# A two-layer hybrid decoder step on one core: warm-up matmuls, order of block 0, tail stores and cache loads

## The chip, the core and the metric

The kernel runs on one core of a Trainium2 chip. The metric is the time of the device in microseconds (us), from the profiler's records or from timed executions.

## What is computed

One inference step of two layers for a prompt group (256 tokens) and a sample group (8 sequences of 4 tokens); both have the same weights and stand side by side as T = 288 columns. The model width is 1024.

```python
x = LN1(alpha*x + 0.5 * SwiGLU_1(x))          # D_FF = 2816
z = x @ w_in                                  # 1024 -> 6144: conv, LRU, query, three gates
y_conv = (cb * conv3(cc * cv)) @ conv_out
y_lru  = (rg_lru(conv4(lx)) * gelu(lg)) @ lru_out
y_att  = attention(q, k_mem, v_mem) @ att_out # 4 heads x 128, 256 memory tokens
m = sum_b sigmoid(g_b) * y_b
x = LN2(alpha*x + m @ w_o)
x = LN3(alpha*x + 0.5 * SwiGLU_2(x))
```

The prompt's keys and values are computed from mem_prompt; those of the samples come from caches, 8 tiles of keys and 8 of values for each layer, 128 x 1024 fp32 (512 KB) each. Outputs are the new x, the prompt's keys and values and the states of the convolutions and of the LRU.

## The kernel before, in words

**Blocks.** Every product with a weight is cut into blocks of 256 output channels; a block n is up to eight 128x256 weight tiles (1 MB), and the class Plan numbers them in the order of the work: F1 and D1 (first SwiGLU), Z (w_in 0 to 11), B (the three branches: gate block, then half-size projection block, four times for each branch), O, F2, D2. A product in fp32 is made of three in fp32r: high by high, high parts of the weights by low parts of x, low parts of the weights by high parts of x (products, L438 to L441). A block so costs 8 x 2 x 3 matmuls of 288 columns.

**Queues.** SP loads the block n into raw (load, L323 to L325) when the low parts of block n-2 are done (lo_ready). ScalarE casts a half block to its high part, whi (L733); VectorE subtracts, wlo (L1030). TensorE waits for lo_ready for each half block and counts pe_half, by one for each half block it has used: after block n it is 2n+2. Each engine works through its list strictly in the order written out in the code, so other vector and scalar work stands between the casts by hand.

**Start (block 0).** first_blocks (L456) does the first two blocks. Their first half is loaded in pieces of two tiles, as is x, on SP's and ScalarE's queues. ScalarE casts a pair of weight tiles, then a pair of x tiles (L742 to L749); VectorE makes the low parts of both (L1042 to L1048) and counts x_ready. TensorE first does eight matmuls of 8 and eight of 256 columns on zeros (L435), then for k = 0, 1, ... four products with xh (high and low weights), two with xl.

**Branches.** For each of the three branches b and four parts i, TensorE does gate(b, i), then project(b, i); with B = plan.at[l]["B"] the gate's block is B + 8b + 2i, the projection's one more. The samples' attention lies between: sample_scores(0 to 3) behind gate(0,1), sample_scores(4 to 7) behind gate(0,3), sample_values(0 to 3) behind project(1,1), sample_values(4 to 7) behind project(1,3). The cache tiles pass through four buffers, kv[b % 4]. Each use counts kv_used. The prompt's attention runs head by head in branch 1: prompt_transposes(i) behind gate(1,i), prompt_values(i) (L654) behind project(1,i). VectorE, for i = 0: the low half of block B+10 (gate_lo), then the copies L1463 of the samples' probabilities into pz, then L1466 (prt), on which prompt_values(0) waits. Ahead of gate(0,3)'s low half it has the LRU's L1410, L1412 and L1413.

**POOL's queue.** For each layer (L410 to L422) POOL sends sixteen cache loads (b = 0 to 7 keys, 8 to 15 values):

```python
for b in range(2 * NS):
    if b == 2:
        pool_e.wait_ge(conv_done, l + 1)
    if b >= BATCH:
        pool_e.wait_ge(kv_used, l * (2 * NS) + b - BATCH + 1)
    ...
    g.dma_start(kv[b % BATCH], cache).then_inc(kv_in[b % BATCH], 16)
    if b == BATCH - 1:
        g.memset(qz_flat, 0.0).then_inc(qz_zero, 1)
    if b == NS + BATCH - 1:
        pool_e.wait_ge(p_prob, l * AH + 1)
        for t in pz_flat:
            g.memset(t, 0.0).then_inc(pz_zero, 1)
```

**Tail.** After the last layer norm ScalarE writes tiles 0 to 4 of x (L866), VectorE tiles 5 to 7 (L1252, counted by y_last). SP stores tiles 0-1, 2-3 and 4-5 (L372), ScalarE's queue tiles 6-7 (L869).

Of the kernel before, what the change touches and what calls it, by code (L numbers as in the profile page):

```python
# [11 lines left out]
P = 128  # L12
HEAD = 128
BC = 256
# [2 lines left out]

ATANH_TERMS = 9
PITCH, SHIFT = 352, 24
WARM_NARROW, WARM_WIDE = 8, 8  # L20
ENDS_ON_ACT = 5

ROW_NAMES = ("ln1_g", "ln1_b", "ln2_g", "ln2_b", "ln3_g", "ln3_b", "conv_w", "lru_conv_w", "lru_conv_b",
# [68 lines left out]
def hybrid_decoder_step(nc, I, O, dims):  # L92
    L, NS, TS, TP, M, D, FF, CK, LK, AH = dims
    T = TP + NS * TS
    DC = LW = D // 2
    KD = D // P
    KB = DC // P
    KF = FF // P
# [30 lines left out]
    with ExitStack() as ctx:  # L129
# [3 lines left out]
        def sem(name):  # L133
            return ctx.enter_context(nc.semaphore(name))
# [99 lines left out]

        first_in = [sem("first_in0"), sem("first_in1"), sem("first_in2")]
        second_in = sem("second_in")
        first_hi, first_lo = sem("first_hi"), sem("first_lo")
        warm_ready = sem("warm_ready")
        hi_ready, lo_ready, pe_half, drained = sem("hi_ready"), sem("lo_ready"), sem("pe_half"), sem("drained")

# [80 lines left out]
        @block.sync  # L321
        def _(sp):
            def load(n, s, src):  # L323
                sp.wait_ge(lo_ready, 2 * n - 2)
                sp.dma_start(raw[:, s, 0:src.shape[1], :], src).then_inc(raw_full[s], 16)  # L325

            def fills(gap):
                for n, f in gap:
                    load(n, n % 2, fill_source(f))

            for l in range(L):
                at = plan.at[l]

                def ffn(k, f0, d0, gap):
                    if l == 0 and k == 1:
                        src = I["ffn1_wg"][0, 0]
                        for c, full in enumerate((*first_in, raw_full[0])):
                            sp.dma_start(raw[:, 0, 2 * c:2 * c + 2, :], src[:, 2 * c:2 * c + 2, :]).then_inc(full, 16)
                        src = I["ffn1_wu"][0, 0]
                        for (k0, k1), full in zip(halves(KD), (second_in, raw_full[1])):  # L340
                            sp.dma_start(raw[:, 1, k0:k1, :], src[:, k0:k1, :]).then_inc(full, 16)
                    else:
                        n = f0 - len(gap)
                        load(n, n % 2, I[f"ffn{k}_wg"][l, 0])
                        fills(gap)
                        load(f0 + 1, (f0 + 1) % 2, I[f"ffn{k}_wu"][l, 0])
                    with sp.Fori(1, PAIRS_F) as i:
                        for s, w in enumerate((f"ffn{k}_wg", f"ffn{k}_wu")):
                            load(f0 + 2 * i + s, (f0 + s) % 2,
                                 I[w][l, bass.ds(i, 1)].rearrange("o p k n -> p (o k) n"))  # L350
                    for b in range(3 * PAIRS_D):
                        j, c = divmod(b, 3)
                        load(d0 + b, (d0 + b) % 2, I[f"ffn{k}_wd"][l, j][:, 8 * c:8 * c + DK[c], :])

                ffn(1, at["F1"], at["D1"], gap(3 * l - 1) if l else ())
                for n, j, f in z_blocks(l):
                    load(n, n % 2, I["w_in"][l, j] if f is None else fill_source(f))
                for b, w in enumerate(("conv_out", "lru_out", "att_out")):
                    for i in range(PAIRS_D):
                        n = at["B"] + 8 * b + 2 * i  # L360
                        load(n, n % 2, I["w_in"][l, 12 + 4 * b + i])
                        load(n + 1, (n + 1) % 2, I[w][l, i])
                for j in range(PAIRS_D):
                    load(at["O"] + j, (at["O"] + j) % 2, I["w_o"][l, j])
                ffn(2, at["F2"], at["D2"], gap(3 * l + 1))


            for p in range(PAIRS_D - 1):
                sp.wait_ge(x_full, KD * (3 * L - 1) + min(2 * p + 2, ENDS_ON_ACT))
                if 2 * p + 2 > ENDS_ON_ACT:  # L370
                    sp.wait_ge(y_last, 2 * p + 2 - ENDS_ON_ACT)
                sp.dma_start(O["y"][:, 2 * p:2 * p + 2, :], x[:, 2 * p:2 * p + 2, :]).then_inc(y_out, 16)  # L372
            sp.wait_ge(k_out, 16 * L)
            sp.wait_ge(v_out, 16 * L)
            sp.wait_ge(col_out, 16 * L)
            sp.wait_ge(y_out, 16 * PAIRS_D)

        @block.gpsimd
        def _(pool_e):
# [17 lines left out]
            for l in range(L):  # L397
                if l > 0:
                    pool_e.wait_ge(bd_psum, l * 8)
                for j, w in enumerate(("lru_wa", "lru_wx")):  # L400
                    for e in range(2):
                        h = P // 2
                        g.dma_start(bd[e * h:(e + 1) * h, j, :, e * h:(e + 1) * h],
                                    I[w][l].rearrange("(k e) a b -> e a k b", e=2)[e]).then_inc(bd_in, 16)
                pool_e.wait_ge(fill_out, plan.fills_done(l, "k"))
                g.dma_start(O["p_mem_k"][l], kt[:, :, :]).then_inc(k_out, 16)
                pool_e.wait_ge(fill_out, plan.fills_done(l, "v"))
                g.dma_start(O["p_mem_v"][l], vt[:, :, :]).then_inc(v_out, 16)

                for b in range(2 * NS):  # L410
                    if b == 2:
                        pool_e.wait_ge(conv_done, l + 1)
                    if b >= BATCH:
                        pool_e.wait_ge(kv_used, l * (2 * NS) + b - BATCH + 1)
                    cache = I["cache_k" if b < NS else "cache_v"][l, b % NS]
                    g.dma_start(kv[b % BATCH], cache).then_inc(kv_in[b % BATCH], 16)
                    if b == BATCH - 1:
# [5 lines that stand above are left out]
                if l + 1 < L:  # L423
                    pool_e.wait_ge(kv_used, (l + 1) * (2 * NS))
                    g.dma_start(mem[:, :, :], I["mem"]).then_inc(mem_in, 16)
                pool_e.wait_ge(col_ready, l + 1)
                g.dma_start(O["cols"][l], cols[:, l]).then_inc(col_out, 16)

        @block.tensor
        def _(pe):  # L430
# [1 line left out]
            pe.wait_ge(consts, 7)  # L432

            pe.wait_ge(warm_ready, 1)
            for cols in (8,) * WARM_NARROW + (BC,) * WARM_WIDE:  # L435
                mm(ps[:, 7, 0:cols], hh[:, KF - 1, 0:P], hh[:, KF - 1, 0:cols], start=True, stop=True)

            def products(out, wh, wl, mh, ml, start, stop):  # L438
                mm(out, wh, mh, start=start, stop=False)  # L439
# [15 lines left out]

            def first_blocks(n):  # L456

                for s, k in ((s, k) for s in range(2) for k in range(KD)):
                    if (s, k) == (0, 0):
                        pe.wait_ge(xh_ready, 1)  # L460
                    elif s == 0:
                        pe.wait_ge(x_ready, k + 1)
                    if s == 0 and k % 2 == 0:
                        pe.wait_ge(lo_ready if k % 4 else first_lo, k // 4 + 1)
# [3 lines left out]
                    for t in range(2):  # L468
# [1 line left out]
                        c = slice(t * P, (t + 1) * P)  # L470
                        mm(out, whi[:, s, k, c], xh[:, k, :], start=k == 0, stop=False)  # L471
                        mm(out, wlo[:, s, k, c], xh[:, k, :], start=False, stop=False)  # L472
                    if (s, k) == (0, 0):
                        pe.wait_ge(x_ready, 1)
                    for t in range(2):
                        last = mm(ps[:, 2 * s + t, 0:T], whi[:, s, k, t * P:(t + 1) * P], xl[:, k, :],
                                  start=False, stop=k == KD - 1)
# [251 lines left out]
        def _(act):  # L729
# [14 lines left out]
            for c in range(PAIRS_D):  # L744
                p = slice(2 * c, 2 * c + 2)
                act.wait_ge((*first_in, raw_full[0])[c], 16)
                s_.copy(whi[:, 0, p, :], raw[:, 0, p, :]).then_inc(hi_ready if c % 2 else first_hi, 1)
                act.wait_ge(x_in[c], 16)
                s_.copy(xh[:, p, :], x[:, p, :]).then_inc(xh_ready, 2)  # L749
            for (k0, k1), full in zip(halves(KD), (second_in, raw_full[1])):  # L750
                act.wait_ge(full, 16)
                split(1, 1, k0, k1)
# [5 lines left out]
            for l in range(L):  # L758
# [77 lines left out]
                def norm(n, l, ln):  # L836
# [25 lines left out]
                    if not more:  # L862
                        gc = ROWS[f"ln{ln + 1}_g"]
                        for k in range(ENDS_ON_ACT):
                            act.wait_ge(normed, KD * q + k // 2 + 1)
                            s_.activation(x[:, k, :], y[:, k, :], ACT.Identity, bias=pts[:, l, bc + k:bc + k + 1],  # L866
                                          scale=pts[:, l, gc + k:gc + k + 1]).then_inc(x_full, 1)
                        act.wait_ge(y_last, KD - ENDS_ON_ACT)
                        s_.dma_start(O["y"][:, KD - 2:KD, :], x[:, KD - 2:KD, :]).then_inc(y_out, 16)  # L869
                        return  # L870
                    for k in range(KD):
                        act.wait_ge(normed, KD * q + k + 1)
# [151 lines left out]
        def _(dve):  # L1024
# [14 lines left out]

            dve.wait_ge(bd_zero, 1)  # L1040
            v.tensor_copy(hh[:, KF - 1, 0:BC], bd[:, 0, 0:2, :].rearrange("p k c -> p (k c)")).then_inc(warm_ready, 1)
            for c in range(PAIRS_D):  # L1042
                p = slice(2 * c, 2 * c + 2)
                dve.wait_ge(hi_ready if c % 2 else first_hi, c // 2 + 1)
                rest(wlo[:, 0, p, :], raw[:, 0, p, :], whi[:, 0, p, :]).then_inc(lo_ready if c % 2 else first_lo, 1)
                dve.wait_ge(x_in[c], 16)
                dve.wait_ge(xh_ready, 2 * c + 2)
                rest(xl[:, p, :], x[:, p, :], xh[:, p, :]).then_inc(x_ready, 2)  # L1048
            for h in range(2):
                lo(1, h)  # L1050
# [517 lines left out]
```

## Time and profile before

| | us |
|---|---|
| median of 3 runs | 1396.47 |
| lowest, highest | 1395.02, 1397.40 |
| the profiled execution | 1396.84 |
| its span | 1394.9 |
| TensorE busy (98% of the span) | 1373.7 |
| VectorE busy (64%) | 894.8 |
| ScalarE busy (48%) | 665.9 |
| POOL busy (2%) | 34.8 |

The span runs from the first to the last record of the profiled execution; its time has about 2 us more around it. Busy times are sums over an engine's instructions. DMA-issuing instructions are not counted as busy. Each instruction of the timeline has its start, its length, its line and, in brackets, how long the engine was idle before it and what ended that.

### The profile page before, as it was taken

To read this page: it belongs to the slowest core of one execution; us is meant where nothing else is said; L and a number is where in the kernel's file an instruction comes from. 1 tells how busy PE (TensorE), PEld (TensorE's weight loads), DVE (VectorE), ACT (ScalarE), POOL (GpSimd) and SP (SyncE) were. 2 spreads that over 40 slices of the span, in tenths; PEclk is the share of its full clock that TensorE was granted. 3 is DMA by queue.
4 is the path that set the end of the run, shared out by engine and by line. 5 is a ranking of instruction groups with operands and counts; after the bars stand their busy time and mean duration, and the time that the engine had idled before them with its cause. 6 is when DMAs were issued, how large, how long until landed. Compare 5 with 4: busy or idle time off the path is not lost.

```text
span 1394.9 us, 25447 instructions
## 1 busy us (share of the span) xinstructions
PE 1373.7 (98%) x10566; PEld 1357.2 (97%) x10566; DVE 894.8 (64%) x1180; ACT 665.9 (48%) x896; POOL 34.8 (2%) x68
## 2 busy tenths in 40 slices
PE   9999999999999999999999999999999999999996
PEld 8999999999899999999999999999998999999996
DVE  5555568496865885554685555585887568655444
ACT  5444446445444664444474444463544455544433
POOL 0100000000101000000000000000001000000000
PEclk9999999999999999999999999999999999999999
DMA  6654444755555454444445544446455453554441
GB/s 241 203 178 157 152 166 160 258 179 178 203 191 204 159 182 157 173 154 162 167 167 181 179 154 143 166 172 228 167 202 204 162 200 129 181 180 153 171 166 57
DMA packets 39998, 243.60 MB, mean 175 GB/s; under 512 B 4577, under 2 KB 4593, under 8 KB 16369
## 3 DMA queue, kind: packets, MB, share of 16 engines
q1 hardware_dynamic: 33264, 219.00, 45.0%
q0 software_dynamic: 5936, 22.01, 4.3%
q10 hardware_dynamic: 720, 1.47, 0.3%
q8 instruction: 59, 0.97, 0.3%
q14 instruction: 19, 0.15, 0.0%
HBM read 238.97 MB, written 3.50 MB: 174 GB/s over the span
## 4 chain that ended last, share of the span: by engine, by line
PE 91%; DVE 4%; DMA 3%; ACT 1%; issue 1%; DVEq 0%
PE ps L440 29%; PE ps L439 29%; PE ps L441 29%; DMA raw<-in_w_in 2%; DVE wlo L1030 1%; PE ps L527 1%; ACT whi L733 1%; PE ps L638 1%; PE ps L631 1%; PE ps L654 1%; PE ps L599 0%; PE ps L623 0%; DMA raw<-in_ffn_wg 0%; PE ps L471 0%; PE ps L472 0%
## 5 line engine op out<-in xcount | busy, mean ns | idle before, releaser
L1030 DVE TENSOR_TENSOR wlo<-raw,whi 128x1024 fp32r<-128x1024 f32 (+1 forms) x450 | 510.1, 1141 | 320.6 <-ACT whi L733 316.4
L733 ACT CAST whi<-raw 128x1024 fp32r<-128x1024 f32 (+1 forms) x446 | 437.2, 987 | 505.1 <-PE ps L441 382.9
L439 PE MATMUL ps<-xh,whi 128*128 128x288 f32 (+1 forms) x2144 | 635.6, 296 | 4.4 <-DVE wlo L1030 3.2
L440 PE MATMUL ps<-xl,whi 128*128 128x288 f32 (+1 forms) x2144 | 631.4, 294 | 0.0
L441 PE MATMUL ps<-xh,wlo 128*128 128x288 f32 (+1 forms) x2144 | 630.5, 294 | 0.0
L439 PEld LDWEIGHTS ps<-xh,whi 128*128 128x128 f32 x2144 | 404.4, 189 | 6.9 <-ACT pool L964 2.9
L440 PEld LDWEIGHTS ps<-xl,whi 128*128 128x128 f32 x2144 | 406.1, 189 | 0.7
L441 PEld LDWEIGHTS ps<-xh,wlo 128*128 128x128 f32 x2144 | 405.5, 189 | 0.0
L439 PE MATMUL ps<-hh,whi 128*128 128x288 f32 (+1 forms) x1088 | 322.0, 296 | 0.0
L440 PE MATMUL ps<-hl,whi 128*128 128x288 f32 (+1 forms) x1088 | 319.4, 294 | 0.0
L441 PE MATMUL ps<-hh,wlo 128*128 128x288 f32 (+1 forms) x1088 | 319.1, 293 | 0.0
L440 PEld LDWEIGHTS ps<-hl,whi 128*128 128x128 f32 x1088 | 206.1, 189 | 0.4
L439 PEld LDWEIGHTS ps<-hh,whi 128*128 128x128 f32 x1088 | 205.2, 189 | 1.2 <-issue 0.8
L441 PEld LDWEIGHTS ps<-hh,wlo 128*128 128x128 f32 x1088 | 205.7, 189 | 0.0
L1100 DVE SCALAR_TENSOR_TENSOR pool<-pool,ps 128x576 f32<-128x576 f32 x41 | 30.9, 753 | 49.9 <-ACT pool L774 49.9
L774 ACT ACTIVATE pool<-ps 128x576 f32<-128x576 f32 x41 | 26.7, 651 | 69.9 <-PE ps L441 69.9
L1106 DVE TENSOR_TENSOR pool<-pool,ps 128x576 f32<-128x576 f32 x44 | 33.1, 753 | 34.6 <-PE ps L441 34.6
L1030 DVE TENSOR_TENSOR hl<-pool,hh 128x576 f32 (+3 forms) x54 | 45.2, 844 | 0.9 <-ACT hh L819 0.2
L1146 DVE SCALAR_TENSOR_TENSOR y<-x,ps 128x576 f32<-128x576 f32 x18 | 13.6, 754 | 33.6 <-PE ps L441 33.6
L791 ACT CAST hh<-pool 128x576 f32 (+1 forms) x44 | 29.7, 675 | 3.2 <-DVE pool L1106 3.2
L860 ACT ACTIVATE xh<-y,pts 128x288 fp32r<-128x288 f32 x40 | 20.4, 532 | 18.9 <-DVE y L1221 18.4
L964 ACT ACTIVATE pool<-ps 128x576 f32<-128x576 f32 x24 | 15.6, 650 | 18.6 <-PE ps L441 18.6
(191 smaller groups left out, 747.5 us busy)
## 6 DMA issues: line engine op xcount, KB each, us to landing
raw<-in_w_in SPq DMA_DIRECT2D x48, 1024.0 KB, 4.9
raw<-in_ffn_wg SPq DMA_DIRECT2D x43, 1024.0 KB, 4.9
raw<-in_ffn_wu SPq DMA_DIRECT2D x43, 1024.0 KB, 4.9
raw<-in_ffn_wd SPq DMA_DIRECT2D x32, 1024.0 KB, 4.9
raw<-in_ffn_wd SPq DMA_DIRECT2D x16, 768.0 KB, 4.1
raw<-in_w_o SPq DMA_DIRECT2D x8, 1024.0 KB, 4.9
raw<-in_w_k_mem SPq DMA_DIRECT2D x4, 1024.0 KB, 5.5
raw<-in_w_v_mem SPq DMA_DIRECT2D x4, 1024.0 KB, 5.7
```

The lines of the kernel that those rows point to most:

```text
L439: mm(out, wh, mh, start=start, stop=False)
L440: mm(out, wh, ml, start=False, stop=False)
L441: return mm(out, wl, mh, start=False, stop=stop)
L527: return mm(ps[:, 4 + kind, 0:T], ones[:, :], tile, start=first, stop=last)
L733: s_.copy(whi[:, s, k0:k1, :], raw[:, s, k0:k1, :]).then_inc(hi_ready, 1)
L774: s_.activation(th[:, :, :], ps[:, 0:2, 0:T], ACT.Tanh, scale=0.5).then_inc(ffn_tanh, 1)
L791: s_.copy(hh[:, bass.ds(i * 2, 2), :], hf[:, :, :]).then_inc(ffn_hi, 1)
L860: return s_.activation(out[:, k, :], y[:, k, :], ACT.Identity, bias=pts[:, l, bc + k:bc + k + 1])
L964: s_.activation(tg[:, :, :], ps[:, 0:2, 0:T], ACT.Tanh, scale=0.5).then_inc(gate_tanh, 1)
L1030: return v.tensor_tensor(out, full, high.bitcast(F32), sub)
L1100: v.scalar_tensor_tensor(sg[:, :, :], th[:, :, :], 1.0, ps[:, 0:2, 0:T], add, mult).then_inc(drained, 1)
L1106: v.tensor_tensor(hf[:, :, :], sg[:, :, :], ps[:, 2:4, 0:T], mult).then_inc(drained, 1)
```

## The change

It has four parts.

1. The warm-up on zeros is seventeen matmuls of 256 columns in place of eight of 8 and eight of 256.
2. In block 0 VectorE casts the first pair of x tiles, as soon as it has landed, in place of ScalarE; TensorE does the four products of high parts for k = 0, 1 first, then the four with the low weights, then the four with the low x; from k = 2 on the order is as it was.
3. The last stores are regrouped: SP stores tiles 0-1, 2-3, 5-6 and 7, ScalarE's queue tile 4.
4. From b = 4 on, of each group of four cache loads the second, third and fourth also wait for pe_half to reach 2n+4, 2n+5 and 2n+6, n being block B+2, B+6 or B+10 for the three groups. 2n+4 is the end of the projection behind gate block n, 2n+5 the middle of the next gate block, 2n+6 its end.

```diff
-WARM_NARROW, WARM_WIDE = 8, 8
+WARM = 17
...
+            def leave(k0, k1):
+                sp.dma_start(O["y"][:, k0:k1, :], x[:, k0:k1, :]).then_inc(y_out, 16)
+
+            for k in range(0, ENDS_ON_ACT - 1, 2):
+                sp.wait_ge(x_full, KD * (3 * L - 1) + k + 2)
+                leave(k, k + 2)
+            sp.wait_ge(y_last, KD - 1 - ENDS_ON_ACT)
+            leave(ENDS_ON_ACT, KD - 1)
+            sp.wait_ge(y_last, KD - ENDS_ON_ACT)
+            leave(KD - 1, KD)
...
+                def spread(b):
+
+                    n = plan.at[l]["B"] + (2, 6, 10)[b // BATCH - 1]
+                    return 2 * n + (0, 4, 5, 6)[b % BATCH]
+
                 for b in range(2 * NS):
                     if b == 2:
                         pool_e.wait_ge(conv_done, l + 1)
                     if b >= BATCH:
                         pool_e.wait_ge(kv_used, l * (2 * NS) + b - BATCH + 1)
+                        if b % BATCH:
+                            pool_e.wait_ge(pe_half, spread(b))
...
-            for cols in (8,) * WARM_NARROW + (BC,) * WARM_WIDE:
-                mm(ps[:, 7, 0:cols], hh[:, KF - 1, 0:P], hh[:, KF - 1, 0:cols], start=True, stop=True)
+            for _ in range(WARM):
+                mm(ps[:, 7, 0:BC], hh[:, KF - 1, 0:P], hh[:, KF - 1, 0:BC], start=True, stop=True)
...
-                for s, k in ((s, k) for s in range(2) for k in range(KD)):
-                    if (s, k) == (0, 0):
-                        pe.wait_ge(xh_ready, 1)
-                    elif s == 0:
+                pe.wait_ge(first_xh, 1)
+                pe.wait_ge(first_hi, 1)
+                for part in range(3):
+                    if part > 0:
+                        pe.wait_ge((None, first_lo, x_ready)[part], part)
+                    for k in range(2):
+                        for t in range(2):
+                            mm(ps[:, t, 0:T], (wlo if part == 1 else whi)[:, 0, k, t * P:(t + 1) * P],
+                               (xl if part == 2 else xh)[:, k, :], start=k + part == 0, stop=False)
+                for s, k in [(0, k) for k in range(2, KD)] + [(1, k) for k in range(KD)]:
+                    if s == 0:
                         pe.wait_ge(x_ready, k + 1)
...
-                act.wait_ge(x_in[c], 16)
-                s_.copy(xh[:, p, :], x[:, p, :]).then_inc(xh_ready, 2)
+                if c > 0:
+                    act.wait_ge(x_in[c], 16)
+                    s_.copy(xh[:, p, :], x[:, p, :]).then_inc(xh_ready, 4 if c == 1 else 2)
...
-                        act.wait_ge(y_last, KD - ENDS_ON_ACT)
-                        s_.dma_start(O["y"][:, KD - 2:KD, :], x[:, KD - 2:KD, :]).then_inc(y_out, 16)
+                        act.wait_ge(x_full, KD * q + ENDS_ON_ACT)
+                        s_.dma_start(O["y"][:, ENDS_ON_ACT - 1:ENDS_ON_ACT, :],
+                                     x[:, ENDS_ON_ACT - 1:ENDS_ON_ACT, :]).then_inc(y_out, 16)
...
+            dve.wait_ge(x_in[0], 16)
+            v.tensor_copy(xh[:, 0:2, :], x[:, 0:2, :]).then_inc(first_xh, 1)
             for c in range(PAIRS_D):
```

## Rows read from the trace of the kernel before

**Rows 1.** The page, busy time of TensorE: us, share of the span, instructions.
```profile
PE 1373.7 (98%) x10566; PEld 1357.2 (97%) x10566; DVE 894.8 (64%) x1180; ACT 665.9 (48%) x896; POOL 34.8 (2%) x68
```

**Rows 2.** TensorE's waits: us in total, times, longest us.
```profile
PE ps L439 <- DVE wlo L1030: 3.2, 2, 2.7
...
PE ps L654 <- DVE pool L1466: 1.9, 2, 1.7
```

**Rows 3.** Timeline of TensorE: start, us, line, form, idle before and releaser.
```profile
355.10 0.37 PE L439 MATMUL ps<-xh,whi 128*128 128x288 f32 x1 [2.73 <-DVE wlo L1030]
...
378.14 0.45 PE L654 MATMUL ps<-pool,vt 128*128 128x256 f32 x1 [0.22 <-DVE pool L1466]
...
1039.92 0.37 PE L439 MATMUL ps<-xh,whi 128*128 128x288 f32 x1 [0.45 <-DVE wlo L1030]
...
1064.51 0.45 PE L654 MATMUL ps<-pool,vt 128*128 128x256 f32 x1 [1.72 <-DVE pool L1466]
```

**Rows 4.** Timeline of SP, issue of blocks B+6 and B+10 in layer 0.
```profile
344.79 0.33 SPq L325 DMA_DIRECT2D raw<-in_w_in  x1
...
369.86 0.33 SPq L325 DMA_DIRECT2D raw<-in_w_in  x1
```

**Rows 5.** DMA issues, last us to landing; from 338, 362, 370, 391, 1026, 1055 us.
```profile
raw<-in_w_in SPq DMA_DIRECT2D x1, 1024.0 KB, 7.8
...
kv_more<-in_cache_v POOLq DMA_DIRECT2D x1, 512.0 KB, 3.4
...
raw<-in_w_in SPq DMA_DIRECT2D x1, 1024.0 KB, 4.8
...
raw<-in_lru_out SPq DMA_DIRECT2D x1, 512.0 KB, 4.4
kv_more<-in_cache_v POOLq DMA_DIRECT2D x1, 512.0 KB, 6.2
...
raw<-in_w_in SPq DMA_DIRECT2D x1, 1024.0 KB, 6.9
...
raw<-in_w_in SPq DMA_DIRECT2D x1, 1024.0 KB, 6.3
```

**Rows 6.** Timeline of TensorE, first product of gate(0,2), layer 0.
```profile
342.81 0.29 PE L439 MATMUL ps<-xh,whi 128*128 128x288 f32 x1
```

**Rows 7.** Timeline of VectorE and ScalarE ahead of gate(0,3), layer 0.
```profile
351.35 0.81 DVE L1413 TENSOR_SCALAR pool<-pool 128x1248 f32<-128x1248 f32 x1
353.73 1.23 DVE L1030 TENSOR_TENSOR wlo<-raw,whi 128x1024 fp32r<-128x1024 f32 x1 [1.57 <-ACT whi L733]
...
352.58 1.04 ACT L733 CAST whi<-raw 128x1024 fp32r<-128x1024 f32 x1 [8.95 <-DMA raw<-in_w_in]
```

**Rows 8.** Timeline of VectorE ahead of gate(0,3), layer 1.
```profile
1037.03 0.81 DVE L1413 TENSOR_SCALAR pool<-pool 128x1248 f32<-128x1248 f32 x1
```

**Rows 9.** Timeline of TensorE, the first transpose behind gate(1,0), layer 0.
```profile
373.92 0.38 PE L690 MATMUL ps<-ident,pool 128*128 128x128 f32 x2
```

**Rows 10.** Timeline of POOL, two cache loads and the zeroing of pz.
```profile
363.60 1.05 POOL L416 DMA_DIRECT2D pool<-in_cache_v  x2
373.89 1.84 POOL L422 MEMSET pool<- 128x1024 f32 x2 [9.23 <-DVE pool L1457]
```

**Rows 11.** Timeline of VectorE ahead of prompt_values(0), both layers.
```profile
376.91 0.48 DVE L1463 COPY pool<-ps 128x128 f32<-128x128 f32 x2
...
1062.14 1.22 DVE L1030 TENSOR_TENSOR wlo<-raw,whi 128x1024 fp32r<-128x1024 f32 x1 [3.47 <-ACT whi L733]
```

**Rows 12.** Timeline of TensorE and VectorE in the first 10 us.
```profile
3.12 3.75 PE L436 MATMUL ps<-hh 128*128 128x8 f32 x16 [3.12 <-DVE hh L1041]
...
8.86 0.76 DVE L1030 TENSOR_TENSOR xl<-x,xh 128x576 fp32r<-128x576 f32 x1
...
9.78 0.30 PE L471 MATMUL ps<-xh,whi 128*128 128x288 f32 x1
```

**Rows 13.** Timeline of the last store.
```profile
1391.58 0.36 ACTq L869 DMA_DIRECT2D out_y<-x  x1
```

More of the change, by code:

```diff
@@ L236, in hybrid_decoder_step @@
         second_in = sem("second_in")
-        first_hi, first_lo = sem("first_hi"), sem("first_lo")
+        first_hi, first_lo, first_xh = sem("first_hi"), sem("first_lo"), sem("first_xh")
         warm_ready = sem("warm_ready")
@@ L365, in _ @@
                 ffn(2, at["F2"], at["D2"], gap(3 * l + 1))
[L368 to L372, printed above, removed]
+            def leave(k0, k1):
[7 more added lines that the diff above has]
+            leave(KD - 1, KD)
             sp.wait_ge(k_out, 16 * L)
@@ L375, in _ @@
             sp.wait_ge(col_out, 16 * L)
-            sp.wait_ge(y_out, 16 * PAIRS_D)
+            sp.wait_ge(y_out, 16 * (PAIRS_D + 1))
         @block.gpsimd
@@ L472, in first_blocks @@
                         mm(out, wlo[:, s, k, c], xh[:, k, :], start=False, stop=False)
-                    if (s, k) == (0, 0):
-                        pe.wait_ge(x_ready, 1)
                     for t in range(2):
@@ L1045, in _ @@
                 rest(wlo[:, 0, p, :], raw[:, 0, p, :], whi[:, 0, p, :]).then_inc(lo_ready if c % 2 else first_lo, 1)
-                dve.wait_ge(x_in[c], 16)
-                dve.wait_ge(xh_ready, 2 * c + 2)
+                if c == 0:
+                    dve.wait_ge(first_xh, 1)
+                else:
+                    dve.wait_ge(x_in[c], 16)
+                    dve.wait_ge(xh_ready, 2 * c + 2)
                 rest(xl[:, p, :], x[:, p, :], xh[:, p, :]).then_inc(x_ready, 2)
```

## The prediction

> **What bounds the kernel now.** I read the page, then who waited for whom on TensorE, then the timelines around the longest waits, then the DMA landings there, then the two ends. TensorE is busy for 1373.7 us of a span of 1394.9 us [rows 1], so only what shortens one of its few waits can move the end. Apart from the start, where it has no work yet, the list of waits has two entries that this change can reach: 3.2 us in two waits of a weight product (L439) for the low parts (L1030), and 1.9 us in two waits of the prompt's first value product (L654) for the vector engine's copy L1466 [rows 2]. The timeline places them: 2.73 us before 355.10 in layer 0 and 0.45 us before 1039.92 in layer 1, both at the gate block w_in[15] (block B+6); 0.22 us before 378.14 and 1.72 us before 1064.51, both before prompt_values(0) [rows 3].
>
> The wait at 355.10 goes back over casts to a weight load: w_in, issued at 344.79 [rows 4], landed 7.8 us later, where the same 1 MB load took 4.8 us in a quiet stretch [rows 5]. Just ahead of it the POOL queue had sent four cache tiles of 512 KB back to back; a single one in a quiet stretch lands after 3.4 us [rows 5]. In layer 1 the same load took 6.9 us behind the same four tiles, and the load of block B+10 (gate(1,1)) took 6.3 us against 4.8 us in layer 0 [rows 5].
>
> **The change part by part.** The sum is made against the profiled execution, 1396.84 us, which lies 0.37 us above the median of 1396.47.
>
> *Block B+6, layer 0.* b=4 still goes out at once; b=5 now waits for project(0,1), which ends at 342.81, b=6 for the first half of gate(0,2), which takes 3.1 us (TensorE's 1373.7 us over its 10566 matmuls is 0.13 us each, and a half block has 24), b=7 for its end, another 3.1 us [rows 1, 6]. So at 344.79 one tile has mostly moved, and two come behind the weights. The price of 512 KB that goes ahead is 4.8 - 3.4 = 1.4 us at most (512 KB more in a load). The weights should land 4.8 to 6.2 us after 344.79, at 349.6 to 351.0; the cast takes 1.04 us, to 352.05 at the latest. VectorE isn't free until L1413 ends at 351.35 + 0.81 = 352.16; its 1.23 us for the low half ends at 353.4, and TensorE starts 0.14 us behind it as before (354.96 to 355.10), at 353.53 [rows 7]. That is 1.57 us earlier, wherever in that interval the load lands; what is late next is L1413. I take **-1.5**, between -1.57 and 0.
>
> *Block B+6, layer 1.* VectorE's L1413 ends at 1037.84 there [rows 8] and would allow 1039.2, but TensorE is only idle for 0.45 us [rows 3]. Where does b=5 fall? TensorE is ready for the block at 355.10 - 2.73 = 352.37 in layer 0, 9.56 us after project(0,1) ends, so in layer 1, ready at 1039.47, that end is at 1029.9. The load is issued at 1039.92 - 2.53 (landing to start, as in layer 0) - 6.9 = 1030.5. So b=5 goes out 0.6 us ahead of the weights, and 4.8 + 1.4 = 6.2 us instead of 6.9 is the likely landing, 0.7 us sooner. I take **-0.4**, between -0.45 and 0.
>
> *Block B+10.* Today all four value tiles are sent at about 362.6, and the weights issued at 369.86 [rows 4] find the queues empty: 4.8 us. After it b=11 follows the end of gate(1,0) at 373.92 [rows 9], b=10 the end of its first half, 3.1 us before that, at 370.8 or 0.9 us behind the weights, and b=9 its start, at 367.6 (6.3 us before its end). If the tile behind the weights shares their bandwidth, they land up to 1.4 us later, and TensorE, idle for 0.22 us already, waits for all of it. The nearest row is a 512 KB weight load at 391.5 with a cache tile 0.3 us behind it: the weights took 4.4 us, the tile 6.2 instead of 3.4 [rows 5]. The later one paid. So I take **+0.3** in layer 0, between 0 and +1.4. In layer 1 the landing of 6.3 us leaves 1.5 us to win, all of it inside the 1.72 us wait. By the layer 0 row minus the same 0.3 that is 1.2; since I can't show that the tiles caused the excess, **-1.1**, between -1.5 and 0.
>
> Beside this stands a rule of the Trainium skill, "DMA: Bandwidth & Descriptors", section on queues, rings and completion order: each DMA engine takes turns between the queues that have work, packet by packet. By it the tile behind the weights does slow them, and the term is +1.4; the row at 391.5 speaks against it. It is a rival below.
>
> *The zeroing of pz (L422).* It stands behind b=11 in POOL's order, so the new wait of b=11 holds it. Today it starts at 373.89 and takes 1.84 us for both halves [rows 10]. Now: gate(1,0) ends at 373.92, about 0.4 us for the last matmul and the wake, 0.53 us for the issue (POOL's row of two tiles takes 1.05 [rows 10]), 1.84 us: about 376.8. VectorE reaches its consumer, L1463, at 376.91 [rows 11]. In layer 1 the gate's end lies as far ahead of TensorE's being ready for L654 as in layer 0 (377.92 - 373.92 = 4.0), at 1062.79 - 4.0 = 1058.8, and the same 2.9 us give 1061.7; VectorE's low half there runs from 1062.14 to 1063.4 [rows 11], or to 1062.2 if the load is 1.2 us faster. Cost **0**, with a margin of 0.1 and 0.5 us; up to +0.6 without it. The value tiles themselves are wanted only after project(1,1), over 10 us later. The third group of tiles (b=12 to 15) has no TensorE wait near it, now or with tiles sent later: 0.
>
> *Block 0.* The sixteen warm-up matmuls took 3.75 us [rows 12]; seventeen wide ones take about as long (1/16 of it, 0.2 us, more), to about 7.0. VectorE casts the first x (its subtraction on the same 576 columns takes 0.76) while ScalarE casts the weights. The twelve products of k = 0, 1 can then start at about 7.0. But k = 2 waits for x_ready 3, the low parts of the second pair of x, which VectorE has at 8.86 + 0.76 = 9.62 behind transfers that aren't touched; today the first product of k = 2 starts at 9.78 [rows 12]. So the twelve products end earlier, and a short wait takes their place. **-0.05**; where the clock comes up later than in this execution, an earlier start is worth up to 0.5, and a change of its timing could cost as much.
>
> *Tail.* Today the last two tiles (288 KB) go out together at 1391.58, behind the third vector op [rows 13]. Now only the last one (144 KB) does, but SP must first issue tiles 5 and 6, two issues in one queue. The same bytes are in flight in the last 3 us. I take **-0.15**, between -0.5 and +0.3.
>
> Sum: -1.5 - 0.4 + 0.3 - 1.1 - 0.05 - 0.15 = -2.9. From 1396.84 that is 1393.9; against the median, with which the result is compared, 1396.47 - 2.9 = **1393.6**.
>
> **The rivals.**
> 1. *The queues take turns* (the skill's rule). B+6 in layer 0 still gains its 1.5, since VectorE is the limit up to a landing of 6.2 us. In layer 1 the load meets b=5 and b=6: -0.2. B+10 costs +1.4 in layer 0 and, at 6.2 instead of 6.3 us, gains 0.1 in layer 1. Sum -1.5 - 0.2 + 1.4 - 0.1 - 0.2 = -0.6: 1395.9. For it: a rule; against it: the tile that paid at 391.5.
> 2. *The excess isn't the tiles'.* A load of block B+10 took 6.3 us some 6 us behind its tiles, so a part of such excess may be scatter. Then only B+6 in layer 0 gains: -1.5 - 0.2 = -1.7: 1394.8.
> 3. *Slower: pz_zero comes last.* If POOL's issue of b=11, the fourth tile in its ring, is held up, or wakes late, each us beyond 376.9 and 1062.2 stands in front of L1463, L1466 and so of L654, in both layers. It decides from 0.1 us on; to lose 2.9 + 2.8 us it has to be about 2.9 us late in each layer, which gives 1396.47 + 2.8 = 1399.3. Against it: POOL's rows of two tiles are 1.05 us wherever I look.
> 4. *More than forecast*: all bounds good, -1.57 - 0.45 - 1.5 - 0.5 - 0.5 = -4.5: 1392.0.
>
> **How the numbers follow.** A measurement of this kernel can tell 0.2%, 2.8 us, from no change, so the forecast stands right at that border. The forecast's case has 0.58, of which a bit over 0.4 beyond -2.8; rival 1 0.18, rival 2 0.12, rival 3 0.05, rival 4 0.07. Faster 0.47, within 0.2% 0.48, slower 0.05. The range takes in rival 4 and rival 1 with half a us of scatter between executions: 1391.6 to 1396.5.
>
> **What would show it.** Right: the L439 wait of 2.73 us shrinks to about 1.2 us and follows L1413 directly; the 0.45 us wait is gone; w_in of B+6 lands in under 6.2 us; L654 waits for under 0.8 us in each layer; b=5, 6, 7 each alone on POOL's timeline. Rival 1: w_in of B+10 at 6 us or more in both layers, the wait before L654 over 1.2 us in both. Rival 3: L1463 is released by the memset L422. In block 0 a short wait of TensorE before k = 2, ended by the low part of x, and k = 2 at 9.7. The prediction is wrong if TensorE's waits shrink as said and the time doesn't, or if the start or the tail moves by over 0.6 us.

## The result and the profile after

The changed kernel takes 1400.08 us (median of 20 runs), the kernel before 1394.86 us in as many runs beside it: a ratio of 1.003, interval 1.002 to 1.0039. It is **slower by 0.3%**, outside the predicted range (1391.6 to 1396.5) and on the side that had a chance of 0.05: a gain of 2.9 us was forecast, and the medians lie 5.2 us apart the other way. A second series of the changed kernel (g4_after below) gave 1.0023, interval 1.001 to 1.0036. Its profiled execution took 1399.52 us with a span of 1397.6; the page gives the busy times, which stand against [rows 1]:

```profile
PE 1373.6 (98%) x10567; PEld 1356.4 (97%) x10567; DVE 895.4 (64%) x1181; ACT 666.9 (48%) x895; POOL 35.4 (3%) x68
```

TensorE is busy as long as before, so the time went into its waits. Its list of waits (us in total, times, longest), against [rows 2]; L1049, L1490 and L1481 are the lines that were L1030, L1466 and L1457, and L451, L671 and L662 were L439, L654 and L645:

```profile
PE ps L671 <- DVE pool L1490: 4.0, 2, 2.4
...
PE ps L451 <- DVE wlo L1049: 2.8, 2, 2.4
...
PE ps L662 <- DVE pool L1481: 0.3, 1, 0.3
```

Before, the first two stood at 1.9 and 3.2. TensorE's timeline places them, against [rows 3] (start, us, line, form, idle before and releaser):

```profile
355.70 0.37 PE L451 MATMUL ps<-xh,whi 128*128 128x288 f32 x1 [2.35 <-DVE wlo L1049]
...
380.98 0.45 PE L671 MATMUL ps<-pool,vt 128*128 128x256 f32 x1 [2.42 <-DVE pool L1490]
...
1057.71 0.40 PE L451 MATMUL ps<-xh,whi 128*128 128x288 f32 x1 [0.42 <-DVE wlo L1049]
...
1067.07 0.45 PE L671 MATMUL ps<-pool,vt 128*128 128x256 f32 x1 [1.56 <-DVE pool L1490]
```

Of the four waits, the one at block B+6 in layer 0 fell from 2.73 us to 2.35, not by 1.5. The one in front of prompt_values(0) in layer 0 rose from 0.22 to 2.42. The 0.45 us at block B+6 in layer 1 are gone, and 0.42 us have come at the next block but one, gate(1,0). The last is 1.72 before and 1.56 after. The landings explain them. First the cache loads on POOL's timeline, layer 0 (b = 5, 6 and 7, b = 9 and 11, and the zeroing of pz):

```profile
344.51 0.53 POOL L428 DMA_DIRECT2D kv_more<-in_cache_k  x1 [4.32 <-PE ps L453]
...
347.64 0.53 POOL L428 DMA_DIRECT2D pool<-in_cache_k  x1 [2.60 <-PE ps L453]
...
350.77 0.53 POOL L428 DMA_DIRECT2D pool<-in_cache_k  x1 [2.60 <-PE ps L453]
...
368.94 0.53 POOL L428 DMA_DIRECT2D kv_more<-in_cache_v  x1 [5.23 <-PE ps L453]
...
375.29 0.53 POOL L428 DMA_DIRECT2D pool<-in_cache_v  x1 [2.64 <-PE ps L453]
...
375.81 1.86 POOL L434 MEMSET pool<- 128x1024 f32 x2
```

Each tile goes out alone; the third and fourth of a group follow the one before by a half block. Then the DMA issues, last column us to landing: w_in of B+6 (issued at 345.79) and b = 6; b = 9, w_in of B+10 (370.49), b = 10 and lru_out; and from layer 1 w_in of B+6 (1032.73) with b = 5, of B+8 (1042.76) and of B+10 (1057.68):

```profile
raw<-in_w_in SPq DMA_DIRECT2D x1, 1024.0 KB, 7.4
pool<-in_cache_k POOLq DMA_DIRECT2D x1, 512.0 KB, 8.0
...
kv_more<-in_cache_v POOLq DMA_DIRECT2D x1, 512.0 KB, 3.7
...
raw<-in_w_in SPq DMA_DIRECT2D x1, 1024.0 KB, 7.0
...
pool<-in_cache_v POOLq DMA_DIRECT2D x1, 512.0 KB, 7.7
raw<-in_lru_out SPq DMA_DIRECT2D x1, 512.0 KB, 7.8
...
raw<-in_w_in SPq DMA_DIRECT2D x1, 1024.0 KB, 5.0
kv_more<-in_cache_k POOLq DMA_DIRECT2D x1, 512.0 KB, 6.0
...
raw<-in_w_in SPq DMA_DIRECT2D x1, 1024.0 KB, 6.9
...
raw<-in_w_in SPq DMA_DIRECT2D x1, 1024.0 KB, 5.9
```

The weights of B+10 in layer 0, issued while b = 9 is still moving and b = 10 about to start, land after 7.0 us instead of 4.8 [rows 5], and the 2.2 us stand whole in TensorE's wait (0.22 + 2.2 = 2.42). The weights of B+6 in layer 0 have b = 5 ahead of them by 1.3 us and b = 6 behind by 1.9 us, and land after 7.4. In layer 1 they do land sooner, 5.0 instead of 6.9 us, but only 0.45 us were to be won there, and the weights of B+8 take 6.9 instead of 5.0. The last of b = 7 is still moving beside them, but that is only 0.11 MB, and a 16 KB packet of instructions lies within the load as well; which of the two costs the 1.9 us is open.

From the issue of the weights of B+10 in layer 0 to their landing (370.49 to 377.49), the POOL queue moves, in packets, MB and share of 16 engines:

```profile
q0 software_dynamic: 196, 0.74, 31.8%
```

That is more than one tile of 512 KB (0.52 MB): parts of b = 9 and of b = 10.

### The profile page after: what moved, and what is told of

Read it like the earlier page. It is cut to its first block, busy times and chain, and to the rows that moved or that the text cites. A ratio compares the mean times of both kernels' runs of the same rounds, so it can differ in the third digit from the quotient of the medians.

```text
span 1397.6 us, 25466 instructions
## 1 busy us (share of the span) xinstructions
PE 1373.6 (98%) x10567; PEld 1356.4 (97%) x10567; DVE 895.4 (64%) x1181; ACT 666.9 (48%) x895; POOL 35.4 (3%) x68
## 4 chain that ended last, share of the span: by engine, by line
PE 89%; DVE 4%; DMA 3%; ACT 1%; issue 1%; SPq 0%; DVEq 0%; ACTq 0%; POOLq 0%
PE ps L452 29%; PE ps L453 29%; PE ps L451 29%; DMA raw<-in_w_in 2%; DVE wlo L1049 1%; ACT whi L750 1%; PE ps L544 1%; PE ps L648 1%; PE ps L671 1%; DMA raw<-in_ffn_wg 1%; PE ps L616 0%; PE ps L655 0%; DVE y L1239 0%; DMA pts<-in_params 0%; PE ps L640 0%
## 5 line engine op out<-in xcount | busy, mean ns | idle before, releaser
L1049 DVE TENSOR_TENSOR wlo<-raw,whi 128x1024 fp32r<-128x1024 f32 (+1 forms) x450 | 510.8, 1142 | 321.6 <-ACT whi L750 320.9
L451 PE MATMUL ps<-xh,whi 128*128 128x288 f32 (+1 forms) x2144 | 635.6, 296 | 4.2 <-DVE wlo L1049 2.8
L451 PEld LDWEIGHTS ps<-xh,whi 128*128 128x128 f32 x2144 | 404.4, 189 | 6.9 <-ACT pool L983 2.6
L451 PE MATMUL ps<-hh,whi 128*128 128x288 f32 (+1 forms) x1088 | 321.9, 296 | 0.0
L451 PEld LDWEIGHTS ps<-hh,whi 128*128 128x128 f32 x1088 | 205.2, 189 | 1.2 <-issue 0.8
L1049 DVE TENSOR_TENSOR hl<-pool,hh 128x576 f32 (+3 forms) x54 | 45.2, 844 | 0.9 <-ACT hh L837 0.2
```

Of the source, the lines that this page charges most:

```text
L1049: return v.tensor_tensor(out, full, high.bitcast(F32), sub)
```

## The experiments

Each is the kernel before with the edit shown, unless it says "on the changed kernel", and was timed beside the kernel before. **The theories**: T1, the tiles spread one by one slow the loads that TensorE waits for (part 4); against it that the start or the end (parts 1 to 3) costs, or that the clock does.

**Which part?** e1_spread has part 4 alone, e2_nospread parts 1 to 3 alone:

```diff
+                        if b % BATCH:
+                            pool_e.wait_ge(pe_half, spread(b))
```

> Only the fourth part of the change, the cache loads one by one, on the kernel before. Theory A: the tiles sent beside a weight load slow it by more than the 1.4 us of their own transfer, so weights for blocks B+6 and B+10 land after 6 to 8 us in both layers, the wait before prompt_values(0) in layer 0 grows from 0.2 to about 2.4 us, and the time is 4 to 6 us above that of the kernel before (ratio about 1.0035). Theory B (the loss sits in the start, by way of TensorE's clock): the ratio is within 0.999 to 1.001. Theory C (only scatter in the landings): ratio 0.999 to 1.001 too, and the landings differ from those of the changed kernel by over 2 us.

Measured: 1400.48 against 1395.19 us, 1.0033 (1.0022 to 1.0045). The whole loss is there.

> The changed kernel with its fourth part taken out again (cache loads back to back, everything else changed). Theory A: the loss is gone, the time is 0 to 1 us below that of the kernel before (ratio 0.9995). Theory B: nearly all of the loss of about 5 us stays (ratio 1.003).

Measured: 1395.38 us, 0.9998 (0.9989 to 1.0007). e3_warm has only the warm-up (`WARM = 17` matmuls of BC columns), e4_block0 only VectorE's cast of the first x and the new order of block 0's twelve products.

> Only the seventeen wide matmuls on zeros. Theory A: ratio 0.9995 to 1.0005; in the profile the spacing of the first products falls from 0.24 to 0.13 us about 2 us earlier, and k = 2 still starts at about 9.4 to 9.8 us. Theory B: 2 to 5 us slower, with a stretch at 0.24 us spacing that the kernel before doesn't have.

Measured: 0.9999 (0.9989 to 1.0008).

> Only the second part: VectorE casts the first x, products of high parts first in block 0; the old warm-up. Theory A: ratio 0.9995 to 1.0005, the first product up to 0.4 us sooner and k = 2 when the low part of x is ready. Theory B: 2 to 5 us slower, with a wait of 0.5 us or more before k = 2 and a later stretch at 0.24 us spacing.

Measured: 0.9995 (0.9986 to 1.0004). Neither moves the time.

**Which tiles?** A table takes the place of spread(b); 0 means no wait beyond the one before:

```diff
+                hold = ((0, 4, 5, 6), (0, 0, 0, 0), (0, 0, 0, 0))
...
+                        at_half = hold[b // BATCH - 1][b % BATCH]
+                        if at_half:
+                            pool_e.wait_ge(pe_half, 2 * (plan.at[l]["B"] + (2, 6, 10)[b // BATCH - 1]) + at_half)
```

This is f1_keys (b = 4 to 7 one by one). f2_values has `((0, 0, 0, 0), (0, 4, 5, 6), (0, 0, 0, 0))`.

> Only the first group of cache tiles (keys, b = 4 to 7) sent one by one. Theory A1 (the loss is made at block B+10, by the second group; at B+6 gain and loss cancel): ratio 0.9995 to 1.0008, w_in of B+6 lands after about 7.5 us in layer 0 and 5 us in layer 1, the wait before prompt_values(0) in layer 0 is 0.2 to 0.5 us. Theory A2 (each group loses alike): ratio about 1.0015.

Measured: 1396.63 against 1395.08 us, 1.0013 (1.0002 to 1.0024). That is nearer to A2 than to A1: the keys lose a little too.

> Only the second group (values, b = 8 to 11) sent one by one. Theory A1: ratio 1.002 to 1.0035, w_in of B+10 lands after 6.7 to 7 us in both layers, TensorE waits 2 us or more before prompt_values(0) in both, and in some executions its granted clock is at 0.5 for a stretch behind such a wait. Theory A2: ratio about 1.0015. If the clock plays no part: at most the 2 us of the wait in layer 0, ratio 1.0015.

Measured: 1399.73 us, 1.0039 (1.0026 to 1.0052). In its trace the weights of B+10 land after 6.5 and 6.7 us, and TensorE waits for 1.91 and 2.13 us before prompt_values(0). The value tiles b = 8 to 11 carry most of the loss. This interval and e1's overlap, so the third group adds nothing that shows.

**Where may a tile lie?** f3_gaps holds the third and fourth tile of both groups to 2n+8, `((0, 0, 8, 8), (0, 0, 8, 8), (0, 0, 0, 0))`, with pz zeroed behind b = 9. f4_late holds all four value tiles to 2n+8, `((0, 0, 0, 0), (8, 8, 8, 8), (0, 0, 0, 0))`, with pz zeroed ahead of them.

> Two tiles of each of the first two groups at once, the other two only after the next projection block but one is done (pe_half 2n + 8), where no weight load is awaited; pz zeroed behind b = 9. If what costs is a tile in flight beside an awaited weight load, loads of B+6 and B+10 land in 4.8 to 5.5 us in both layers, the wait at B+6 in layer 0 is about 1.2 us and follows L1413, that before prompt_values(0) under 1 us in both layers, ratio 0.998 to 0.9995. If sending tiles later is bad in itself, ratio over 1.001.

Measured: 1396.81 us, 1.0016 (1.0006 to 1.0026). The weights of B+6 land as hoped, after 4.9 and 4.8 us, and so do those of B+10 in layer 0 (4.8), not in layer 1 (6.3). The list of waits of its profiled execution (1402.87 us, well above its median) shows what came instead:

```profile
PE ps L628 <- DMA pool<-in_cache_k: 3.4, 2, 2.0
```

Key tiles b = 6 and 7 of layer 1, sent together at 1041.98 right ahead of the weights of B+8, take 7.7 and 8.8 us, and the scores wait for them, 1.41 and 2.01 us. In layer 0, where the same two tiles go out 1.5 us ahead of the weights, no score waits for them.

> Only the second group changed: all four value tiles held until the projection block of gate(1,0) is done, pz zeroed before them; no tile moves within 15 us ahead of the load of B+10. If the 6.3 to 7.0 us of that load in layer 1 are the tiles' doing, it lands in 4.8 to 5 us, the wait before prompt_values(0) in layer 1 falls from about 2 to 0.5 us, ratio 0.999. If they are not, it still takes over 6 us in layer 1 and the ratio is 0.9995 to 1.0005.

Measured: 1395.78 us, 1.0006 (0.9997 to 1.0015). No tile moves beside the weights of B+10 in layer 1, yet they take 6.3 us, as in the kernel before. The DMA queues from their issue to their landing (queue, kind: packets, MB, share of 16 engines) in f4_late:

```profile
q1 hardware_dynamic: 282, 1.55, 67.9%
q8 instruction: 1, 0.02, 0.9%
...
raw<-in_w_in SPq DMA_DIRECT2D x1, 1024.0 KB, 6.3
```

and in the kernel before for the same block of layer 0, where the load takes 4.8 us:

```profile
q1 hardware_dynamic: 198, 1.27, 72.7%
q0 software_dynamic: 54, 0.17, 8.7%
```

In layer 1 one packet of 16 KB of instructions lies within the load; in layer 0 none does. The share 0.9% of 16 engines over 6.3 us comes to 0.9 us, if one engine carried it. In one trace the packet has moved away: in g3_best (below), with its four value tiles sent together as before, none lies within this load. From its issue to its landing:

```profile
q0 software_dynamic: 19, 0.05, 3.2%
...
raw<-in_w_in SPq DMA_DIRECT2D x1, 1024.0 KB, 4.9
```

So the excess can go although the tiles stay. But a packet within a load is not enough for it: in g1_keys66 one lies within the load of B+6 in layer 0, and that takes 4.8 us. That the packet is the cause is argued, not shown.

**The landings of fifteen traces** (before, after and the runs here but g2_after_busy and g3_best), w_in, us from issue to landing, grouped by how the tiles near it are sent:

| load | four together | one by one | held out of the way |
|---|---|---|---|
| B+6, layer 0 | 7.8 5.4 5.5 7.0 7.0 6.6 | 7.4 5.8 7.7 6.8 7.5 | 4.9 4.8 5.1 5.1 |
| B+6, layer 1 | 6.9 6.7 7.0 6.7 7.3 7.2 | 5.0 4.9 4.9 4.8 4.8 | 4.8 4.8 4.7 4.8 |
| B+8, layer 1 | 5.0 4.8 4.8 5.3 5.4 5.0 | 6.9 5.8 6.9 6.2 5.1 | 7.5 5.8 5.7 5.7 |
| B+10, layer 0 | 4.8 4.8 5.0 4.9 4.8 4.9 4.9 4.7 | 7.0 6.7 6.7 6.5 6.4 | 4.8 4.9 |
| B+10, layer 1 | 6.3 7.0 6.6 6.8 6.3 6.8 6.2 6.4 | 5.9 7.2 6.7 6.7 6.0 | 6.3 6.3 |

Three rows are plain: B+10 in layer 0 pays 1.8 us for the spread (means 4.85 and 6.66), B+6 in layer 1 gains 2.1 us, and B+10 in layer 1 doesn't care. B+6 in layer 0 takes 6.6 us in the mean with four together and 7.0 one by one: no gain.

Of the two traces left out of the table, g2_after_busy (one by one) has 8.2, 7.6, 5.0, 6.1 and 6.6 in these rows, and g3_best (b = 6 and 7 held, the values together) 4.7, 5.0, 6.4, 4.9 and 4.9. Two of these break a row. B+10 in layer 1 takes 4.9 in g3_best, as said. B+6 in layer 1 takes 7.6 in g2_after_busy: there b = 5 goes out 1.1 us ahead of the weights, in the five others 0.2 us behind them. That gain hangs on where b = 5 falls.

**The version that follows.** g1_keys66 leaves all as before but for b = 6 and 7, held to 2n+6: behind the landing of the weights of B+6 and ahead of those of B+8.

```diff
+                hold = ((0, 0, 6, 6), (0, 0, 0, 0), (0, 0, 0, 0))
```

> The kernel before with only b = 6 and 7 held, both to the end of gate(0,2) (pe_half 2n + 6), behind the landing of w_in of B+6 and ahead of the load of B+8. If a tile costs only where it is in flight beside an awaited weight load: w_in of B+6 lands in about 4.9 us in both layers, its wait in layer 0 is 0.8 to 1.3 us behind L1413, none in layer 1, no wait for a cache tile, ratio 0.9985 to 0.9998. If holding tiles is bad in itself: over 1.0005.

Measured: 1394.51 against 1396.16 us, 0.9984 (0.9974 to 0.9995). In this series it is faster than both kernels, if by little; h3_all_keys66 and h2_best8 below, with the same hold, don't repeat the gain. Its list of waits:

```profile
PE ps L659 <- DVE pool L1471: 2.8, 2, 2.4
...
PE ps L444 <- DVE wlo L1035: 1.2, 1, 1.2
```

and the timelines of POOL, VectorE and TensorE ahead of gate(0,3) in layer 0:

```profile
349.93 1.05 POOL L421 DMA_DIRECT2D pool<-in_cache_k  x2 [10.07 <-PE ps L446]
...
351.54 0.80 DVE L1418 TENSOR_SCALAR pool<-pool 128x1248 f32<-128x1248 f32 x1
...
352.38 1.23 DVE L1035 TENSOR_TENSOR wlo<-raw,whi 128x1024 fp32r<-128x1024 f32 x1
...
353.75 0.37 PE L444 MATMUL ps<-xh,whi 128*128 128x288 f32 x1 [1.24 <-DVE wlo L1035]
```

With the weights there after 4.8 us the low half follows L1418 (L1413 before) directly, and the wait is 1.24 us: what the prediction had forecast of part 4 at this block, to the tenth.

h3_all_keys66 is the changed kernel with this hold in place of part 4.

> The changed kernel with its fourth part replaced by g1's (only b = 6 and 7 held, to the end of gate(0,2)); warm-up, block 0 and tail as changed. Since those three together made no difference (e2), ratio as g1: 0.998 to 0.9995. If they interact with the loads: outside of that.

Measured: 1394.65 against 1395.66 us, 0.9994 (0.9983 to 1.0005). Its interval and g1's overlap: the hold is worth between nothing and 0.2%, and a gain is not shown. Exchanging part 4 for it takes the whole loss of the changed kernel away.

**The clock.** In the profiled execution of e1_spread, 1405.55 us and the slowest of its twelve, the granted clock of TensorE falls behind three of its waits (stretch, us, busy us of TensorE, its weight load, VectorE, ScalarE, GpSimd with counts, granted clock, DMA share, GB/s):

```profile
356.00:358.00 2.00, 2.00 (x10) 2.00 (x10) 2.00 (x4) 0.93 (x2) 0.00 (x0) 0.50 0.27 43
...
384.00:386.00 2.00, 2.00 (x8) 1.82 (x8) 2.00 (x5) 0.00 (x0) 0.00 (x0) 0.50 0.77 291
388.00:390.00 2.00, 2.00 (x17) 2.00 (x16) 0.72 (x3) 1.05 (x1) 0.00 (x0) 1.00 0.30 117
1073.00:1075.00 2.00, 2.00 (x9) 1.91 (x9) 2.00 (x5) 0.00 (x0) 0.00 (x0) 0.50 0.84 270
```

At 0.50 (1.2 GHz) eight to ten matmuls pass in 2 us, at 1.00 (2.4 GHz) seventeen. The waits ahead of the three low stretches were 2.56, 2.09 and 2.31 us. A low stretch lasts about 3.4 us, so it costs 1.7 us of products.

Such a wait doesn't always bring one. In the changed kernel's own profile the clock stays up behind 2.35 and 2.42 us (its row from 381 us, right behind the second):

```profile
381.00:383.00 2.00, 2.00 (x10) 1.79 (x11) 2.00 (x3) 0.66 (x2) 0.00 (x0) 1.00 0.10 16
```

So it does in the kernel before, behind 2.73 us. Over all seventeen traces TensorE has 22 waits of 1.8 to 2.9 us between its start and its end; a low stretch follows 14 of them (one, in f3_gaps, is of 7 us), and none lies elsewhere, but for the last 15 us. The length of the wait doesn't tell the two kinds apart: 1.81 us had one behind it, 2.94 us had none.

To part the two costs, g4_after repeats the changed kernel, g2_after_busy adds to it twenty products of the identity with itself, unused, just before prompt_values(0) in both layers, so that TensorE doesn't stand still there, and g3_best adds such products to g1_keys66 (sixteen at prompt_values(0) of layer 1, and eight ahead of gate(0,3), in both layers).

```diff
+                        pe.wait_ge(p_exp, l * (NT * AH) + NT)
+                        for _ in range(20):
+                            mm(ps[:, 4, 0:P], ident[:, :], ident[:, :], start=True, stop=True)
```

> The changed kernel again, unaltered, on the chip of the other three: ratio 1.0030 to 1.0040, mean clock 0.995 to 0.997.

Measured: 1400.61 us, 1.0023 (1.001 to 1.0036). Its clock, the same columns:

```profile
380.50:383.00 2.50, 2.50 (x11) 2.41 (x10) 2.50 (x5) 0.00 (x0) 0.00 (x0) 0.50 0.91 298
384.00:386.00 2.00, 2.00 (x17) 2.00 (x16) 0.87 (x3) 0.91 (x3) 0.00 (x0) 1.00 0.67 246
```

> The changed kernel with twenty small products of the identity on a free bank of PSUM, between project(1,0) and prompt_values(0) in both layers, where TensorE waits for 1.6 to 2.4 us. They bring nothing to the result. If a part of the loss is TensorE's clock, which falls behind such a wait, they keep it up: 1 to 2.5 us faster than the changed kernel (ratio to the kernel before 1.0015 to 1.0025), mean granted clock 0.997 in most executions, no stretch at 0.5. If the loss is only the waits: the same as the changed kernel, or slower.

Measured: 1405.27 us, 1.0058 (1.0045 to 1.0071), in six runs. The groups of TensorE's instructions from 378 to 385 us (line, form and count, busy us, mean ns, idle before) show why:

```profile
L716 PE MATMUL ps<-ident 128*128 128x128 f32 x40 | 4.6, 275 | 0.0
```

The twenty products (each in two passes) took 4.6 us where the wait was 2.4. The experiment cost more than the wait that it filled.

> g1 with sixteen such products at prompt_values(0) of layer 1 and eight ahead of gate(0,3). If the clock counts in the kernel before too (its profile shows none of it, but some of its executions have a mean clock of 0.996 or less): ratio 0.997 to 0.999. If not: like g1.

Measured: 1399.22 us, 1.0021 (1.001 to 1.0031), outside both forecasts: the same flaw. The sixteen took 3.7 us and the eight 1.9 us in each layer, 7.6 us in all, where the waits that they were to fill came to 3.7 us in g1_keys66's trace. h1_after_busy8 and h2_best8 put it right with eight products, on the changed kernel in both layers and on g1_keys66 in layer 1.

> The changed kernel with eight products of the identity ahead of prompt_values(0) in both layers. In g2 twenty of them took 4.5 us, 0.22 us each, 2 us longer than the wait they were to fill; eight take 1.8 us and fit in waits of 2.1 to 2.9 us. If TensorE's clock carries a part of the loss: 1 to 2 us faster than the changed kernel (ratio to before about 1.002 where the changed kernel has 1.003), mean granted clock over the executions 0.9970 in place of 0.996. If only the waits count: as the changed kernel, and the mean clock is no higher.

Measured: 1399.77 against 1395.66 us, 1.0027 (1.0017 to 1.0037). The wait at L671 has gone from its list, but the one at B+6 (2.4 us) hasn't, nor the low stretch behind it, and the mean granted clock of its executions is 0.9962 against 0.9960 and 0.9958 for the changed kernel.

> g1 (two key tiles held to the end of gate(0,2)) with eight such products ahead of prompt_values(0) of layer 1, where it waits for 1.7 to 2.4 us. If the clock counts: 0.3 to 1 us faster than g1, ratio 0.9975 to 0.9985. If not: 0.998 to 0.999.

Measured: 1395.65 us, 0.9999 (0.999 to 1.0008), above both forecasts. Filling a wait buys nothing that can be measured. What the clock costs isn't settled by these four.

It can be bounded by grouping all executions by their mean granted clock. The 32 of the changed kernel have 3 at .998 (1395.5 us in the mean), 6 at .997 (1397.5), 14 at .996 (1400.2) and 9 below (1402.0). The 127 of the kernel before in its four series with experiments have 28 at .998 and 82 at .997 (1395.2 both), 11 at .996 (1397.3) and 6 below (1398.9). At the same clock, .997, the changed kernel is 2.3 us slower, with six executions that reach from 1394.9 to 1399.6; it is at .996 or below far more often.

## Why the prediction was wrong

**What the 5 us consist of.** The three waits listed above come to 7.1 us in the changed kernel's trace, 5.6 in g4_after's and 7.7 in e1_spread's, 6.8 in the mean; with four tiles together they are 5.1 (before), 4.1 (e2), 4.4 (e3) and 4.0 (e4), 4.4 in the mean. That is +2.4 us, and the 2.3 us at equal clock are of that size. The mean granted clock fell from .9970 to .9959, and 0.0011 of 1397 us is 1.5 us of product time, about one low stretch of 1.7 us more in each execution (an estimate). About 1.3 us of the 5.2 are not placed. The waits are shown by part 4 alone, and by its removal; the clock's share is an association only.

**The step that failed is "Block B+10"**, layer 0: +0.3, between 0 and +1.4. It was +2.2 us in the profiled execution and 1.8 in the mean of the landings, above the upper bound. The sum priced one tile, b = 10 behind the weights. It left out b = 9, which it had placed 2.3 us ahead of them, though by its own 3.4 us for a tile that one was still in flight. In the trace b = 9 goes 1.6 us ahead of the weights and b = 10 1.6 us behind, and 0.74 MB of tiles move beside them. At the sum's own price, 1.4 us for 512 KB, that is 2.0 us (an estimate) against the 2.2 measured. The other four traces of the table with the values one by one have 0.68, 0.64, 0.60 and 0.58 MB there, 1.8 to 1.5 us by the same estimate, and their weights landed 1.9 to 1.5 us later than the 4.85. So by these landings the number of tiles counted was wrong, not the price of one; no run moved b = 9 or b = 10 alone.

The row at 391.5 was taken for more than it holds. It is right for a tile that goes out directly behind the weights: at B+6 in layer 1 b = 5 goes 0.2 us behind them, 0.27 to 0.30 MB of it move beside them, they take 4.8 to 5.0 us in five traces, and b = 5 takes 5.9 to 6.0. It says nothing of a tile ahead. Two of its readings were off as well: the "single" tile of 3.4 us and the tile of 6.2 us are both the first of four sent back to back. A tile really alone, b = 8 of layer 0, takes 3.4 to 3.9 us in six traces.

The Trainium skill's rule ("DMA: Bandwidth & Descriptors", section on queues, rings and completion order), that each DMA engine takes turns between the queues with work, is borne out by B+10 in layer 0 in all five traces with the values one by one, 6.4 to 7.0 us, but B+6 in layer 1 hardly pays for the tile beside it. The page gives no price, and rival 1 gave no more than +1.4 because it too counted b = 10 alone.

**Block B+6, layer 0** (-1.5): 7.4 us instead of at most 6.2, so -0.4 in the profiled execution and nothing in the mean of the table. The bound counted b = 5 as "mostly moved" and b = 6 as free, the same error; 0.93 MB moved beside these weights. Besides, the 7.8 us of the profiled execution was the upper end of a load that takes 5.4 to 7.8 us in six traces, so most of the 2.73 us wait was never there to win on average. **Layer 1** (-0.4) came out, 5.0 us and no wait, but in part by luck: the sum had b = 5 0.6 us ahead of the weights and a landing after 6.2 us. It went out 0.2 us behind them; in g2_after_busy, where it went 1.1 us ahead, the load took 7.6 us and TensorE waited for 2.39 us. What was left out is the weights of B+8, 1.9 us later: 0.42 us at gate(1,0), and 0.33 at L662. **B+10, layer 1** (-1.1): wrong, it was -0.2. The load takes 5.9 to 7.2 us in sixteen of the seventeen traces however the tiles are sent, even with none near it (f4_late), as rival 2 had it; the exception is g3_best's 4.9.

**A term was missing**: the granted clock behind a wait of some 2 us. Nothing in the sum stood for it, and so nothing in the upper end of the range, 1396.5.

**What held.** pz_zero cost nothing: POOL was through at 377.67, and VectorE's timeline shows L1487 (L1463 before) straight behind the low half, which itself waited for the cast:

```profile
378.62 1.23 DVE L1049 TENSOR_TENSOR wlo<-raw,whi 128x1024 fp32r<-128x1024 f32 x1 [4.16 <-ACT whi L750]
379.76 0.48 DVE L1487 COPY pool<-ps 128x128 f32<-128x128 f32 x2
380.15 0.68 DVE L1490 COPY pool<-ps 128x512 f32<-128x512 f32 x1
```

So rival 3 didn't come about; the slow side came from a transfer, not from a wait of POOL. In block 0 the short wait before k = 2 came as described, on the low part of x, in the timeline of TensorE:

```profile
3.12 3.96 PE L448 MATMUL ps<-hh 128*128 128x256 f32 x17 [3.12 <-DVE hh L1060]
...
9.38 0.40 PE L490 MATMUL ps<-xh,whi 128*128 128x288 f32 x1 [0.69 <-DVE xl L1049]
```

It starts 0.4 us earlier than in [rows 12], and e2 to e4 show no time from it. The tail's -0.15 is below what e2_nospread can tell, 0.1%. Rival 1 came nearest in its mechanism, with 1395.9 us; it still credited B+6 in layer 0 with its 1.5 us. Rival 3's 1399.3 us is the nearest number, by a mechanism that wasn't at work.

## What to carry to other kernels

A background transfer costs what it does to the load that someone waits for, so spreading is not neutral. Count every tile that is in flight when the load goes out, those ahead of it too. Then put it behind the landing of an awaited load and ahead of the next issue (b = 6 and 7 at 2n+6), and check both neighbours and the tile's own deadline (f3_gaps). Before a wait is counted as a gain, see whether it is as long in other executions: one profile had the load that mattered at the top of its scatter. A wait of TensorE of some 2 us may cost more than itself, through the clock, by 1.7 us here where a low stretch followed.

## What the runs showed of the hardware

- A 1 MB load with one 512 KB tile of the other queue 1.6 us ahead and one 1.6 us behind it (B+10 in layer 0) took 6.4 to 7.0 us instead of 4.7 to 5.0, with 0.58 to 0.74 MB of tiles moving beside it. Tiles suffered as much: b = 10 took 7.7 us, where b = 8 alone took 3.4 to 3.9. With a tile only 0.2 us behind it (B+6 in layer 1) the load took 4.8 to 5.0 us, and the tile 5.9 to 6.0.
- In layer 1 the load of B+10 took 5.9 to 7.2 us in sixteen traces, in f4_late with a 16 KB packet of instructions in flight beside it and no tile; in g3_best, without such a packet, it took 4.9. Other loads took 4.8 us with one.
- The granted clock stood at 0.50 for some 3.4 us behind 14 of 22 waits of 1.8 to 2.9 us, and TensorE passed 8 to 10 matmuls of this kernel in 2 us there instead of 17.
